# Two-layer hybrid decoder step: the sample's state sums as 64x64 blocks with repeated columns, its attention ahead of the state's output, and a later clearing of the prompt's states

## What is computed

```
def wkv_step(s, inp):
    r, w, k, v, kk, a = inp
    sa = jnp.einsum("bhvk,bhk->bhv", s, -kk)
    s = s * w[:, :, None, :] + sa[..., None] * (kk * a)[:, :, None, :] + v[..., None] * k[:, :, None, :]
    return s, jnp.einsum("bhvk,bhk->bhv", s, r)
...
s = jnp.einsum("bqkgd,bskd->bkgqs", qg, keys, preferred_element_type=jnp.float32) * (A_HEAD_DIM ** -0.5)
o = sink_attention(s, mask, sinks, vals, "bkgqs,bskd->bqkgd")
...
y = jnp.concatenate([ya, yb, yc], axis=-1) @ lp["w_out"]
x = x + gate_m[:, None] * rmsnorm(y, lp["norm_post"])
```

## Time and profile before

| | us |
|---|---|
| median of 3 runs | 2876.16 |
| lowest and highest run | 2868.34, 2879.36 |
| the profiled execution | 2875.11 |
| its span, first to last instruction | 2873.3 |

### The profile page before, as it was taken

How to read it: one execution, slowest core, us unless ns; L and a number is a source line. 1 busy time by engine, 2 the same in 40 slices (tenths; PEclk the granted TensorE clock), 3 DMA queues, 4 the chain that set the end, 5 groups by cost and what they waited for, 6 DMA issues and landing times.

```text
span 2873.3 us, 63497 instructions
## 1 busy us (share of the span) xinstructions
PE 2750.8 (96%) x25044; PEld 2011.8 (70%) x25044; DVE 1715.9 (60%) x4635; ACT 1343.5 (47%) x3140; POOL 254.7 (9%) x357
## 2 busy tenths in 40 slices
PE   6999999999999999998679999999999999999986
PEld 5777777777777777776457777777777777777753
DVE  2666666666666666656146666666666666666654
ACT  2554444545555444544125554444545554444432
POOL 0000111101100011100000100111011100111000
PEclk7999999999999999999679999999999999999997
DMA  9200000000000000003550000000000000000002
GB/s 360 83 19 22 23 24 24 9 24 24 24 24 17 24 24 24 9 17 119 149 209 16 24 17 24 24 23 25 9 24 25 24 18 22 24 23 16 9 16 44
DMA packets 62136, 119.18 MB, mean 41 GB/s; under 512 B 15232, under 2 KB 35200, under 8 KB 61568
## 3 DMA queue, kind: packets, MB, share of 16 engines
q1 hardware_dynamic: 55792, 113.64, 11.9%
q10 hardware_dynamic: 6032, 1.12, 0.2%
HBM read 96.34 MB, written 18.41 MB: 40 GB/s over the span
## 4 chain that ended last, share of the span: by engine, by line
PE 91%; DVE 4%; issue 2%; DMA 2%; ACT 2%; SPq 0%; POOL 0%; DVEq 0%; POOLq 0%; ACTq 0%
PE G L506 17%; PE G L632 16%; PE M L854 15%; PE G L501 8%; PE M L501 5%; PE M L681 5%; PE M L497 4%; PE M L694 3%; PE G L748 2%; PE G L512 1%; PE M L660 1%; PE M L730 1%; PE G L497 1%; DVE Q L1611 1%; PE M L758 1%
## 5 line engine op out<-in xcount | busy, mean ns | idle before, releaser
L506 PE MATMUL G<-hT,w_in 128*128 128x128 f32 x4224 | 506.8, 278 | 3.3 <-issue 3.3
L506 PEld LDWEIGHTS G<-hT,w_in 128*128 128x128 f32 x4224 | 494.7, 194 | 21.4 <-issue 16.4
L632 PE MATMUL G<-hT,w_in 128*128 128x256 f32 (+1 forms) x2048 | 497.1, 385 | 0.0
L854 PE MATMUL M<-w_out,yT 128*128 128x512 f32 x1024 | 452.5, 595 | 2.8 <-DVE yT L1751 2.8
L632 PEld LDWEIGHTS G<-hT,w_in 128*128 128x128 f32 x2048 | 360.4, 189 | 64.7 <-issue 12.3
L854 PEld LDWEIGHTS M<-w_out,yT 128*128 128x128 f32 x1024 | 192.7, 191 | 220.6 <-issue 219.1
L501 PE MATMUL G<-w_in,hT 128*128 128x512 f32 x512 | 244.2, 609 | 0.0
L1611 DVE TENSOR_TENSOR Q<-Q,M 64x256 f32<-64x256 f32 x320 | 133.8, 418 | 130.5 <-PE M L694 127.3
L681 PEld LDWEIGHTS M<-W 64*64 64x64 f32 x4608 | 147.6, 135 | 24.3 <-issue 24.3
L681 PE MATMUL M<-W 64*64 64x64 f32 x4608 | 162.7, 219 | 0.0
L1371 POOL TENSOR_TENSOR RA<-RA,small 128x1024 f32<-128x1024 f32 x32 | 60.6, 1894 | 1134.2 <-DVE small L1663 1134.2
(11 more groups left out here) (455 smaller groups left out, 4557.4 us busy)
## 6 DMA issues: line engine op xcount, KB each, us to landing
w_in<-in_w_in SPq DMA_DIRECT2D x8, 2048.0 KB, 15.2
w_out<-in_w_out SPq DMA_DIRECT2D x2, 4096.0 KB, 18.8
G<-in_x_prompt SPq DMA_DIRECT2D x16, 512.0 KB, 3.6
x_mid<-RA SPq DMA_DIRECT2D x16, 512.0 KB, 2.9
G<-x_mid SPq DMA_DIRECT2D x16, 512.0 KB, 3.3
out_y_prompt<-RA SPq DMA_DIRECT2D x16, 512.0 KB, 2.8
xa<-in_x_prompt SPq DMA_DIRECT2D x15, 512.0 KB, 3.7
xa<-x_mid SPq DMA_DIRECT2D x15, 512.0 KB, 3.8
```

Of the source, the lines that this page charges most:

```text
L506: last = mm(out[0:width, :], Win[:, k, col:col + width], H[:, k, :], start=k == 0, stop=k == KC - 1)
L632: last = mm(out, Win[:, k, col:col + P], moving, start=k == 0, stop=k == KC - 1)
L854: last = mm(o[:, :], yT[:, k, :], Wout[:, k, 512 * h:512 * h + 512], start=k == 0, stop=k == KC - 1)
```

## The change

- **Clearing.** `cleared(l + 1)`, and with it the modulation of the next layer, moves on VectorE from the projection to just ahead of its wait for `pv_mm`.
- **Sums.** `sa_mm`, `vb_mm` and a new `y_mm` are 32 products each over 64 rows. For the first two the stationary operand is one column repeated 64 times (`to_broadcast`), the moving one a 64x64 block: of the identity for `vb_mm`, of the old state for `sa_mm`. For `y_mm` the new state's block is stationary and the receptance's one column moves. The diagonal form, the multiplications by kk and r over 128x1024 and the last reduction fall away. The decayed state gets a place of its own (`dSw`, in hT), and the value's part is added to it before `sa` is there.
- **Attention.** Its query rows are made ahead of the bonus and the key, the scores go to M1 between `sa_mm` and `y_mm`, ScalarE's exponentials ahead of the RG-LRU's root.
- **SP.** `xa` (dT2 is no longer in it) and rope are loaded ahead of the state.

```diff
@@ block.sync @@
                 if mixed:
                     load_x2(d["x_mid"][P:2 * P, :])
+                    sp.dma_start(xa[:, :], d["x_mid"][0:P, :]).then_inc(L["x_in"], 16)
+                    load_rope(0, (l + 1) * NT)
                     sp.wait_ge(L["modT_mm"], 1 + MODG)
                 sp.dma_start(dS, d["wkv_s"][l]).then_inc(smp["kv_in"], 16)
...
-                if l < DEPTH - 1:
-
-                    sp.wait_ge(smp["dve"], AT("y", l))
-                    sp.dma_start(xa[:, :], d["x_mid"][0:P, :]).then_inc(L["x_in"], 16)
-                    load_rope(0, (l + 1) * NT)
@@ block.tensor @@
+                units = [(u + 8 * (r ^ w), r) for w in range(2) for u in range(8) for r in range(2)]
+
+                pe.wait_ge(smp["in_small"], (l + 1) * 64)
+                pe.wait_ge(smp["dve"], AT("xs", l))
+                for u, r in units:
+                    last = mm((M4, G0)[u // 8][half[r], HD * (u % 8):HD * (u % 8) + HD],
+                              dx[half[r], 4 + u // 8, u % 8:u % 8 + 1].to_broadcast([HD, HD]), dcon("stack")[half[r], :],
+                              start=True, stop=True)
+                last.then_inc(smp["pe"], 1)
...
                 pe.wait_ge(smp["dve"], AT("skk", l))
                 pe.wait_ge(smp["act"], AT("gates", l))
                 pe.wait_ge(smp["act"], AT("kknorm", l))
-                mm(M2[:, :], ones, dT1[:, 0:512], start=True, stop=True)
-                mm(M3[:, :], ones, dT1[:, 512:1024], start=True, stop=True).then_inc(smp["pe"], 1)
...
+                pe.wait_ge(smp["kv_in"], (l + 1) * 96)
+                S3 = dS.rearrange("p (u v) -> p u v", v=HD)
+                for u, r in units:
+                    last = mm((M2, M3)[u // 8][half[r], HD * (u % 8):HD * (u % 8) + HD],
+                              dkk[half[r], u:u + 1].to_broadcast([HD, HD]), S3[half[r], u, :], start=True, stop=True)
+                last.then_inc(smp["pe"], 1)
...
                 for b in range(B):
-                    last = mm(M4[0:64, 0:P + 1], stB[:, 64 * b:64 * b + 64], KTs[:, b, :], start=b == 0, stop=b == B - 1)
+                    last = mm(M1[0:64, 0:P + 1], stB[:, 64 * b:64 * b + 64], KTs[:, b, :], start=b == 0, stop=b == B - 1)
+                last.then_inc(smp["pe"], 1)
+
+                pe.wait_ge(smp["dve"], AT("s_new", l))
+                for u in range(16):
+                    for r in range(2):
+                        last = mm((M2, M3)[r][half[r], u:u + 1], S3[half[r], u, :], dx[half[r], u // 8, u % 8:u % 8 + 1],
+                                  start=True, stop=True)
                 last.then_inc(smp["pe"], 1)
@@ block.scalar @@
+                act.wait_ge(smp["dve"], AT("neg", l))
+                A(dm[0:64, 5:6], dm[0:64, 3:4], ACT.Exp)
+                A(Pd[0:64, :], M1[0:64, 0:P + 1], ACT.Exp, bias=dm[0:64, 2:3], scale=SCALE,
+                  accum_out=dm[0:64, 4:5]).then_inc(smp["act"], 1)
                 act.wait_ge(smp["dve"], AT("lru_t", l))
                 A(dth[:, :, :], dth[:, :, :], ACT.Sqrt, scale=-1.0).then_inc(smp["act"], 1)
@@ block.vector, the sums @@
+                tt(Sw, S3, over(f2(dw[:, :, :]), 2, HD), ALU.mult)
+                dve.wait_ge(smp["pe"], AT("vb_mm", l))
+                tt(A3[:, 0:8], m3(M4), over(kb[:, 0:8], 2, HD), ALU.mult)
+                dl(tt(A3[:, 8:16], m3(G0), over(kb[:, 8:16], 2, HD), ALU.mult))
+                dl(tt(Sw, Sw, A3, ALU.add))
...
+                dve.wait_ge(smp["pe"], AT("sa_mm", l))
                 tt(A3[:, 0:8], m3(M2), over(ab[:, 0:8], 2, HD), ALU.mult)
                 dl(tt(A3[:, 8:16], m3(M3), over(ab[:, 8:16], 2, HD), ALU.mult))
-                dve.wait_ge(smp["pe"], AT("vb_mm", l))
-                dl(tt(S3, S3, A3, ALU.subtract))
-                tt(A3[:, 0:8], m3(M4), over(kb[:, 0:8], 2, HD), ALU.mult)
-                dl(tt(A3[:, 8:16], m3(M5), over(kb[:, 8:16], 2, HD), ALU.mult))
-                signal(tt(S3, S3, A3, ALU.add), "s_new")
-                signal(tt(A3, S3, over(f2(dx[:, 0:2, :]), 2, HD), ALU.mult), "sr")
-                dve.wait_ge(smp["pe"], AT("sr_mm", l))
-                st = over(dcon("stack"), 1, 8)
-                tt(C3[:, 0:8], m3(M2), st, ALU.mult)
-                dl(tt(C3[:, 8:16], m3(M3), st, ALU.mult))
-                signal(red(dyv[:, :], C3, AX_X, ALU.add), "y")
+                signal(tt(S3, Sw, A3, ALU.subtract), "s_new")
...
+                dve.wait_ge(smp["pe"], AT("y_mm", l))
+                cp(dyv[half[0], :], M2[half[0], 0:16])
+                signal(cp(dyv[half[1], :], M3[half[1], 0:16]), "y")
```

86 lines of the change are left out of this document (35 added, 51 removed).

## The result

| | before | after |
|---|---|---|
| median, us | 2874.41 | 2828.05 |
| lowest and highest run | 2868.34, 2879.36 | 2823.62, 2829.47 |
| the profiled execution | 2875.11 | 2828.5 |
| its span | 2873.3 | 2826.6 |

The ratio of the medians is 0.9837 (95% interval 0.9814 to 0.986): 46 us faster, against 49 forecast (2826.8).

A forecast was written before the change was run, and what follows sets the result against it. TensorE, with 91% of the last chain, bounds the kernel, so gains come where it waits. 21.6 + 13.8 + 14.0 = 49.4 us off the span 2873.3 gives 2823.9; adding 1.8 and 1.05, 2826.8 us (range 2815 to 2843, own 2818 to 2836).

The forecast's parts named there:

- Part 1: Layer 0's projection: clearing states later lets the second copy follow at once, gaining 21.6 us.
- the hole: Layer 0's projection: TensorE waits 14.8 us for a copy queued behind the clearing; the half clock after it costs 6.8.
- The chain: Each layer, first use of the projection to the output product: 27.1 us, from 40.91 in layer 0 and 41.15 in layer 1.
- the 34 ns: Three block sums: price per 64x64 record at full clock, from L681 of the loop; 64 records take 2.2 us.
- The rule on weight loads: Block sums: the skill page's 53 ns per 64-column load, if serial 3.4 us a sum at either clock; not adopted.
- Part 4: SP's queue: reloading xa and rope ahead of the state's load costs nothing, with a slack of 2 to 5 us.
- parts 2 to 4: Both layers' chains: block sums, earlier attention and reordered loads, gaining 13.8 us in layer 0 and 14.0 in layer 1.
- (a): Projection and the sums sa and y: the clock stays low, 6.8 us plus 3.6 a layer, total 2841; chance 0.17.
- (b): Block sums: a pair of blocks costs 0.22 us, only 3.1 us gained per layer, total 2848; chance 0.05.
- (c): Layer 0: the state lands late because xa and weights share transfer engines, costing 12.5 us, total 2839; chance 0.08.
- (d): Layer 0's projection: the wait moves to a small load and gives back the clearing's gain, total 2848; chance 0.04.
- (e): Block sums: products do not overlap, about 0.22 us a record, 14 us a sum; 14.8 us slower, 2891; chance 0.02.

The follow-up runs named there:

- e1: Kernel before with only the state clearing moved ahead of VectorE's wait for the product with the values: 2856.88 us against 2872.37.
- e2: Changed kernel with the clearing put back behind the first copy of the projection: 2843.38 us, ratio to before 0.9888.
- e8: Changed kernel run once more, unaltered, for a second trace: 2823.75 us, ratio to before 0.9831.
- e3: Changed kernel with the reload of xa and its rope table put back behind the step y on SP: 2845.18 us, ratio to before 0.9894.
- e4: Changed kernel with attention scores, maximum and exponentials put back behind the state's output and ScalarE's root: 2841.04 us, ratio to before 0.9884.
- e5: Changed kernel with each sum's blocks ordered upper row half first, then lower, instead of in turn: 2847.26 us, ratio to before 0.9917.
- e6: Changed kernel with six spare 128x128 products in TensorE's gaps after the state's output: 2828.36 us, ratio to before 0.9851.
- e11: Changed kernel with attention normalisation ahead of the state's output, gates' products in bank M0 and three wide spare products: 2825.02 us, ratio to before 0.9834.
- e9: Kernel before with only the attention's scores, maximum and exponentials moved earlier, old sums and clearing kept: 2863.8 us, ratio to before 0.9969.

## Why the prediction was right

**Part 1, 21.6 us.** The stretch gained 21.3 in the two profiled executions, which looks like a hit, and e1 and e2 show that it is half luck: alone or undone, the part moves the median by 15. The step that was mis-sized is the reading of the hole and of the half clock behind it from one execution. The hole is 9.9, 14.8 or 15.7 us long, and the half clock behind it lasted 5 us in e2 and about 15 in the kernel before.

**The chain, 27.1 us in each layer.** Measured 26.19 and 26.10, and 27.54 and 26.81 in e8. Step by step in layer 1, from the first use: the first sum is released after 10.48 us (forecast 10.5, by the gates), takes 2.0 us (2.8; the clock had risen a microsecond ahead of it, at about 2796.5, where I had it rise during it), the new state is done after 15.2 us (16), the output takes 2.03 us (2.2), from there to the copies of the transposes 3.5 us (3.5), from these to the output product 5.3 us (5.3). The 2.0 us of the first sum are partly luck: in layer 0 of e8, the same program, it took 3.44. The value's broadcast ran at half clock and took 3.6 us, inside its bounds of 2.2 and 4.3, and was done 1.5 us ahead of the gates. The reason behind the 34 ns was not known to me: I took L681's row as the price of a shape, and it is the price of a shape whose halves and banks alternate, as this kernel's blocks do. Had the change placed its blocks half by half, my forecast would have been some 20 us too low, and nothing in it would have said so.

**The rule on weight loads.** The Trainium skill ("TensorE: Matmul & The Clock Gate", "LDWEIGHTS (loading the stationary operand)") gave 53 ns for 64 columns. The trace has 56 ns a record at half clock and 31 at full clock with the halves in turn, so the serial reading, 3.4 us a sum at either clock, does not hold at the upper level. At the lower one the sum takes about that (3.44 to 3.6 us), though in each half the records are 104 ns apart there and not 53. For the output my estimate from the Trainium skill ("TensorEngine Tiling (Array Packing)", "Instruction Overhead") was 1.6 us; measured 2.03. The other half of what it says, that one moving column costs as much as sixty, the trace bears out: 32 ns a record with one and 31 with 64. The number of moving columns doesn't set that price here.

**Part 4, nothing.** Right for what I looked at (VectorE takes the state at 1420.1 without a wait, the late store is hidden under L503), and wrong as a judgement of the part. I asked only what the move costs, not what the old place would have cost once the rest had become faster. By e3 it would have been 16 us. The forecast didn't need the term, as the change moves the reload; but the whole gain does.

**The sum.** The three terms came out at 51.1 in place of 49.4, and 5.0 us were lost ahead of them, where executions of one program lie 7 us apart (e8). By the medians, parts 2 to 4 without part 1 (e2) bring 29.0 us, forecast 27.8 (by the ratio, 0.9888, it is 32), and part 1 adds 15 to 17, where I had 21.6. That the total lies within 3 us of the forecast rests on errors of a few us that offset each other: part 1 gave less, the rest somewhat more.

**Rivals.** (a) did not happen in the projection, nor in the sums of the first trace after; in e8 and in e2 to e4 one of the first sums did run at half clock and cost 1.3 to 1.4 us, and in e4 `y` did in both layers. So it is real, in single sums and not in all. (b), (c) and (d) did not. (e) has its mechanism, though: records do follow one another if nothing lets them overlap (e5), at 104 ns each at half clock and 59 at the full one, and not 220.

## What to carry to other kernels

Small products on part of the array's rows are cheap only in pairs: write them so that neighbours use different row halves (and, as here, different banks, since no run separates the two), and check the spacing of the records, not the duration of one. When a chain gets shorter, ask of everything that is issued behind it, loads of the next stage above all, whether it would still be in time from its old place. And take a stall's length, and the half clock behind it, from several traces before it goes into a sum.

## What the runs showed of the hardware

- Two 64x64 records in different row halves overlap: 31 to 32 ns a record at the upper clock and 56 at the lower one, against about 59 and 104 with neighbours in the same half (after, e5). Neighbours in different halves also had different accumulator banks here. With one moving column in place of 64 the price is the same, 32 ns.
- TensorE's granted clock fell while its records stood back to back: 0.66 and then 0.50 in 2804 to 2808 of e6, with 2.00 us busy in each 2. Six spare products of 128x128 did not hold it, and three wide ones in e11 shortened neither chain.
- The same program's clock rises and falls at different places. In layer 1 it fell at about 2806.7 in the first trace after, 9 us after the first sum's start, and in e8 within the output itself (0.67 over 2798 to 2800), 6 us after. In layer 0 the first sum ran at the upper level in one (2.08 us) and at the lower one in the other (3.44). Together this is worth 0.7 to 1.4 us a chain. Product L851 of layer 0 took 10.13 us in the first, at a granted clock of 0.69, and 7.11 in the second, at 1.00.
- Six stores of small tiles (64 KB and less) let VectorE wait 12.9 us (e9), 17.0 (before) and 18.8 (e2) for the last of them, 1 KB: 6 us apart from one execution to the next.
